# Attention units of a head pair in the order of widths 256, 512, 384, 128

## What is computed

```python
def block(args):                      # latent attention
    qi, bi = args
    s = jnp.einsum('bqhd,bkhd->bhqk', qi, k).astype(jnp.float32) * scale
    q_chunk = (bi * Q_BLOCK + jnp.arange(Q_BLOCK)) // CHUNK
    mask = key_chunk[None, :] <= q_chunk[:, None]
    s = jnp.where(mask[None, None], s, NEG_INF_2)
    p = jax.nn.softmax(s, axis=-1).astype(v.dtype)
    return jnp.einsum('bhqk,bkhd->bqhd', p, v)
```

## Time and profile before

| what | value |
|---|---|
| time, median of 3 executions | 3009.59 us (3006.89 to 3018.76) |
| profiled execution, its own time | 3008.26 us |
| its span, first to last instruction | 3006.5 us |
| mean granted TensorE clock | 0.908 |
| `natt`, from its first scores to its last DVE instruction | about 160 us |
| `matt`, `batt` | about 59 and 54 us, twice each |

### The profile page before, as it was taken

How to read it: one execution, slowest core, us unless ns; L and a number is a source line. 1 busy time by engine, 2 the same in 40 slices (tenths; PEclk the granted TensorE clock), 3 DMA queues, 4 the chain that set the end, 5 groups by cost and what they waited for, 6 DMA issues and landing times. The chain is left out here.

```text
span 3006.5 us, 34777 instructions
## 1 busy us (share of the span) xinstructions
PE 2516.3 (84%) x13054; PEld 1962.6 (65%) x13054; DVE 1236.6 (41%) x2604; ACT 978.8 (33%) x1575; POOL 758.6 (25%) x214
## 2 busy tenths in 40 slices
PE   6996888788992987997995689896998789896998
PEld 4773777566771765666773547675887647675886
DVE  3534555446445306766544372322122271312122
ACT  2323212214541114753543332422223332422222
POOL 2430000123341320011333202233442203234441
PEclk8997999888995987998998789998999899998999
DMA  4350000017883233113886302223321302123221
GB/s 104 98 223 8 1 1 1 29 47 252 280 270 112 71 86 122 50 56 114 279 280 211 88 28 71 71 71 101 98 84 65 88 29 84 58 84 97 92 81 63
DMA packets 225097, 304.40 MB, mean 101 GB/s; under 512 B 52304, under 2 KB 139872, under 8 KB 224944
## 3 DMA queue, kind: packets, MB, share of 16 engines
q1 hardware_dynamic: 222656, 294.16, 30.4%
q0 software_dynamic: 2304, 8.39, 0.7%
HBM read 270.95 MB, written 31.56 MB: 101 GB/s over the span
## 5 line engine op out<-in xcount | busy, mean ns | idle before, releaser
L159 POOL TENSOR_TENSOR branch_weights_wl<-branch_weights_wf,branch_weights_wh 128x2048 fp32r<-128x2048 f32 (+1 forms) x66 | 301.2, 4564 | 786.6 <-ACT branch_weights_wh L153 786.6
L153 ACT ACTIVATE branch_weights_wh<-branch_weights_wf 128x2048 fp32r<-128x2048 f32 (+1 forms) x66 | 125.0, 1894 | 422.2 <-PE bprojc_acc L201 131.4
L201 PE MATMUL merge_acc<-xh,branch_weights_wh 128*128 128x512 f32 x384 | 153.7, 400 | 19.8 <-PEq L72 19.8
L201 PE MATMUL merge_acc<-xh,branch_weights_wl 128*128 128x512 f32 x384 | 152.5, 397 | 0.0
L201 PE MATMUL merge_acc<-xl,branch_weights_wh 128*128 128x512 f32 x384 | 151.4, 394 | 0.0
L159 POOL TENSOR_TENSOR nsa_weights_wl<-nsa_weights_wf,nsa_weights_wh 128x2048 fp32r<-128x2048 f32 x13 | 59.8, 4599 | 275.8 <-ACT nsa_weights_wh L153 275.8
L1556 PE MATMUL exp_ps_y<-rt_wf,exp_ht 128*128 128x512 f32 x256 | 117.2, 601 | 3.9 <-ACT exp_ht L1600 3.9
L1410 POOL TENSOR_TENSOR rt_wl<-rt_wf,rt_wh 128x2048 fp32r<-128x2048 f32 x16 | 82.6, 5164 | 129.4 <-ACT rt_wh L1406 129.4
L159 POOL TENSOR_TENSOR in_weights_wl<-in_weights_wf,in_weights_wh 128x2048 fp32r<-128x2048 f32 x16 | 75.3, 4705 | 129.9 <-ACT in_weights_wh L153 110.9
L201 PE MATMUL gproj_acc<-xh,in_weights_wh 128*128 128x512 f32 x256 | 101.1, 395 | 3.7 <-POOL in_weights_wl L159 3.7
L2723 DVE TENSOR_TENSOR merge_prod<-merge_gate,merge_b 128x512 f32<-128x512 f32 x32 | 21.9, 684 | 199.4 <-PE merge_b L2667 199.4
(11 more groups left out here) (615 smaller groups left out, 6710.0 us busy)
## 6 DMA issues: line engine op xcount, KB each, us to landing
branch_weights_wf<-w_in SPq DMA_DIRECT2D x56, 1024.0 KB, 5.1
rt_wf<-moe_w_down SPq DMA_DIRECT2D x32, 1024.0 KB, 5.4
in_weights_wf<-gdn_w_in SPq DMA_DIRECT2D x16, 1024.0 KB, 5.6
rt_wf<-moe_w_gate SPq DMA_DIRECT2D x32, 512.0 KB, 7.4
rt_wf<-moe_w_up SPq DMA_DIRECT2D x32, 512.0 KB, 8.1
moe_rows<-rt_y SPq DMA_DIRECT2D x64, 256.0 KB, 2.1
moe_rows<-gproj_zeros SPq DMA_DIRECT2D x1, 12288.0 KB, 35.8
merge_bwf<-w_branch SPq DMA_DIRECT2D x12, 1024.0 KB, 5.0
```

Of the source, the lines that this page charges most:

```text
L153: act.activation(self.h[u][:, :, 0:self.cols(b)], self.s.f[u][:, :, 0:self.cols(b)], ACT.Copy).then_inc(self.s.hi_ready, 1)
L159: pool.tensor_tensor(self.l[u][:, :, 0:self.cols(b)], self.s.f[u][:, :, 0:self.cols(b)], self.h[u][:, :, 0:self.cols(b)].bitcast(F32), ALU ...
L201: mm = pe.matmul(self.acc[:, s, 0:cols], lhs[:, P * s:P * s + P], rhs, start=(u == 0 and k == 0 and n == 0), stop=(u == 1 and k == HALF - ...
```

## The change

The tiles of a pair are taken in the order i = 1, 3, 2, 0, so the widths come as 256, 512, 384, 128, in all five stages; in `natt` each twice, for the two branches. Two conditions that recognised the first unit of a pair by i == 0 now go by its place. No instruction is added or removed, and each has the size that it had.

```diff
+    TILES = (1, 3, 2, 0)
+
     def unit(self, u):
 
-        return u // self.pair_units, u % self.pair_units // self.nb, u % self.nb, P * (u % self.pair_units // self.nb + 1)
+        i = self.TILES[u % self.pair_units // self.nb]
+        return u // self.pair_units, i, u % self.nb, P * (i + 1)
+
+    def first(self, u):
+
+        return u % self.pair_units == 0
...
         hp, i, b, width = self.unit(u)
         pe.wait_ge(self.copied, u + 1)
-        if i == 0 and b == 0 and hp >= 2:
+        if self.first(u) and hp >= 2:
             pe.wait_ge(self.o_read, hp - 1)
...
-                if i == 0 and b == 0:
+                if self.first(n):
                     if self.mt is None:
                         dve.wait_ge(self.b_loaded[h % 4], 16 * (h // 4 + 1))
```

## The result

The changed kernel takes 2995.23 us (median of 8 executions, 2991.47 to 3002.47) against 3013.47 for the kernel before beside it (8, 3006.89 to 3018.76): ratio 0.9942, 95% interval 0.9929 to 0.9955, which is 17.5 us faster (18.2 between the two medians). The forecast was 8.0 us, inside 0.5%. The sign held; the size was twice as large, and faster by over 0.5% had been given 0.13. That it held owes something to luck.

The account below looks back on a forecast made before the run. PE nearly bounds natt; batt and matt pairs are chains from engine to engine. natt -2.0, matt -3.6 and batt -2.4 sum to -8.0 us, giving 3001.6 us for the median; range 2992 to 3010.

Parts of the forecast that it names:

- The chain through a pair: Between pair ends in batt and matt: 0.15 us less per pair, DVE waiting for ACT's exponential instead of PE.
- The pair of natt: One pair of eight units in natt, where PE is nearly the bound: 0.17 us less per pair.
- Fill: At each stage's start, first finish later: by 1.0 us in natt, 0.9 in batt, 0.3 in matt.
- Drain: At each stage's end, last distance shorter: by 2.0 us in natt, 1.8 in each matt and batt stage.
- The granted clock inside the pairs: PE's clock within pairs: no change taken, since PE's share stays; one stretch at the lower level costs 1.57 us.
- the rival (PE standing longer brings the clock down): At pair ends, PE stands longer; a lower-clock stretch in each of 24 pairs costs 37.7 us, net +29.7; chance 0.04.
- The stretches between: Parts of the kernel outside the five attention stages, between barriers: claimed not to move, 0 us.
- The prediction's own tests: In traces: batt pairs 10.7 us, natt 18.9, batt's last below 9, first finish 0.3 to 1.0 later, DVE's wait moved.
- more than that: All stages: natt closes its gaps, drains shorten, six half-clock stretches go; 22 us faster, about 2987; chance 0.12.
- slower: At pair ends: PE's longer standing brings a lower-clock stretch into each of 24 pairs, +29.7 us, about 3039; chance 0.04.

Follow-up runs that it names:

- first-pair experiment: New order in the first pair of the matt and batt stages alone, all else rising, against the kernel before: ratio 1.001 (1.0002 to 1.0019).
- last-pair experiment: New order in the last pair of each of the five stages alone, all other pairs rising, against the kernel before: ratio 0.9961, 11.8 us faster.

## Why the prediction came out as it did

**The chain through a pair** was right in kind. In `batt` and `matt` the stall moved from DVE waiting for PE to ACT's exponential of the 512 unit, as laid out: the profile after shows the wait of 0.47 us for ACT, no idle time ahead of `y`, and PE's wait of 2.02. The size was 0.15 and is 0.27 in `batt` (10.58) and 0.32 in `matt` (11.79).

**The pair of natt.** Forecast 0.17 less, measured 0.02 more. PE is busy 18.13 of 19.05, and its gaps are as long as before in sum (0.92 for 0.85). The room of 7.3 us that the share of weight loads (11.70 of 19.05) seemed to leave was not there: new, rising and falling orders stay within 0.04 us. The Trainium skill (Perfetto Trace Analysis, Identifying the Most-Contended Engine) would judge PE's headroom by that share; for this stage the rows of PE's starts were the better guide.

**Fill.** This step failed. The term for `matt` was +0.3, and it is -0.8 and -1.4; for `batt` +0.9, and it is -0.3 and 0.0; for `natt` +1.0, and it is +1.8. The prediction took the lower clock for the same in both orders. In `matt` the clock came up behind wide first scores, with no pause of PE, about 3.5 us sooner, counted from the stage's start. The first-pair experiment shows it in both layers. For `natt` and `batt`, I did not take the fill apart.

**Drain.** Forecast 1.8 in each `matt` and `batt`, 2.0 in `natt`; measured 2.8 and 2.4 in `matt`, 2.1 and 1.9 in `batt`, 2.0 in `natt`. `natt` and `batt` were met. In `natt` the last distance is 15.8 in every trace with the new order at the end. In `matt` and `batt` it moves with the clock, from 7.6 at clock 1.00 to 10.2, and the 2.8 of `matt` in layer 0 was a favourable draw: 0.1 in the other four traces. The last-pair experiment, at 11.8 us, shows that the drain is the largest part by itself.

**The granted clock inside the pairs** is the term that was mis-sized. "I take no change there, since PE's share in a pair stays as it is" was wrong both ways. `matt` lost a slow pair in each stage, 1.9 us each against its new pair of 11.79. `batt` got three slow pairs, 1.5 each. The sign of the rival (PE standing longer brings the clock down) was right for `batt` alone, where standing grew from 1.40 to 2.02. Filling part of the stand removed the slow pairs in `batt` in the new order (none in 8 distances, two kernels, against 5 of 8 without) and in `matt` rising (none in 4, one kernel, against one or two in each rising stage without): for these, PE's standing is shown to be the cause. The Trainium skill (TensorE: Matmul & The Clock Gate, HAM oscillation) ties the fall to PE idling between bursts, in its own case for some 3 to 5 us at a time. The traces agree in the idling, and show the fall with shorter stands, 0.8 to 2.0 us.

By terms, in us, forecast then measured between the two traces (rounded, so the first row is off by 0.1):

| stages | fill | pairs | drain | together |
|---|---|---|---|---|
| natt | +1.0, +1.8 | -1.0, +0.1 | -2.0, -2.0 | -2.0, 0.0 |
| matt, both | +0.6, -2.2 | -0.6, -4.4 | -3.6, -5.2 | -3.6, -11.8 |
| batt, both | +1.8, -0.2 | -0.6, +3.6 | -3.6, -4.0 | -2.4, -0.6 |

The stretches between were put at 0 and give -3.3; in sum -8.0 and -15.7.

**The prediction's own tests.** The wait ahead of `y` and the last distance of `batt` below 9 came true; `natt`'s distance of 18.9 did not, nor a first finish later by 0.3 to 1.0 (1.8 later in `natt`, as before or up to 1.4 earlier elsewhere). And it had called itself wrong if a pair's distance moved by over half a us: those of `batt` moved by 1.2 to 1.3 in three of four cases, and the third of `matt` by 1.9. The right sign and a time inside the range hide that the fill came out with the wrong sign, and that the clock, put at nothing, moved pairs both ways.

**The rivals.** Nearest in size came "more than that", 22 us, by its drains (11.2 for 9.2) and by fills that cost nothing in sum where it had booked 3.4. `natt` closed no gaps, and the slow pairs went from `matt` (two) and came to `batt` (three). For "slower", the prediction took PE's share of 0.855 as that of the pair with the slow stretch; it is that of the pair beside it, and the slow one has 11.87 of 13.68, 0.87.

**What stays open.** In `matt` the new order stands longer at the pair's end (1.51 for 1.18) and yet has no slow pair in 16 distances, in four kernels. A rising pair also has a second wait of PE (0.59), so the sum of PE's waits in a pair is 1.8 rising, 1.5 new and 0.5 falling, which would fit the slow pairs of `matt`, but for the last-pair experiment: its third pairs have waits of 0.76 and 0.59, 1.35 together, and are slow (14.1) in both layers. In `batt` the sums are 2.2, 2.0 and 1.8, and slow pairs are 5 of 20 rising (five kernels), 5 of 8 new, 0 of 4 falling, which does not follow the sum. The longest wait (1.4, 2.0, 1.4) fits better there, and not in `matt`. So no single number for the stand decides. For the new order in `matt` alone the spans differ by 4.4 us (3006.5 to 3002.1) and the medians by 14.5. That is a matter of which executions were profiled: 5.3 us below the median before, 4.9 above it in the experiment, together the missing 10.1. In its trace `natt`, rising in both, begins 2.9 us later and has its first finish at 28.4 for 26.8, and the last distance of `matt` in layer 0 is 10.2. Open stays where in the five stages or around them the other executions spent their time.

## What to carry to other kernels

Lay out the chain through a pipeline's boundary before booking the time of a shortened step: of 1.07 us saved on PE, 0.3 came out of each pair, because another unit's exponential was next. End a pipelined stage on its smallest unit: it paid 2.0 us or more in `natt` in every trace, and in the new order up to 3 in `matt` and `batt`, though next to nothing where the clock fell for long in the drain. Where TensorE is not full, look at the granted clock pair by pair: in some pairs a stand of 1 to 2 us was followed by a loss of 1.5 to 1.6 us, and repeating a matmul that fits into the stand bought 8 us in the old order in the timed executions, 3.2 of them seen in the `matt` stages of its trace.

## What was not expected of the hardware

- Doing a matmul three times made the kernel faster: 0.9972 with the order unchanged. In the third pair of `matt` the granted clock was 1.00 instead of 0.88.
- A delay of 2.5 us on DVE at one pair's end cost 8.5 us in that stage, as the clock behind it fell to 0.76 and 0.70.
- With wide first matmuls `matt` reached the upper clock level earlier (5.5 us behind the first scores for 8.9), so the order with more to do at the start had its first pair done sooner, by 0.8 and 1.4 us.
